# ScalarE's exponential ahead of its copy, and ScalarE writing the outputs of two of the five attention kinds

## What is computed

```python
o_a = _nsa(...)   # 8 heads of 64: per query g0*compressed + g1*selected + g2*window
o_b = _fox(...)   # 8 heads of 64: softmax(q k^T * scale + c_q - c_k) v, "forget gated"
o_m = _memory_xattn(...)   # 4 heads of 128 over 256 memory rows
x = x + (g_0 * (silu * o_a) @ w_a + g_1 * (silu * o_b) @ w_b + g_2 * (silu * o_m) @ w_m) @ w_out
```

## Time and profile before

| | |
|---|---|
| median of 3 runs | 3017.97 us (3016.29 to 3022.12) |
| profiled execution | 3021.99 us, its span 3020.5 us |
| TensorE matmul busy | 2976.1 us (99%) |
| VectorE busy | 1497.1 us (50%) |
| ScalarE busy | 807.1 us (27%) |
| GpSimd busy | 1939.0 us (64%) |
| granted clock, both attention stages | 1.00 |

### The profile page before, as it was taken

One profiled execution on the slowest core, in us unless ns is written; L12 is line 12 of the kernel. 1 busy time (PEld: TensorE's weight loads), 2 busy tenths in 40 slices (PEclk: granted clock), 3 DMA queues, 4 the chain that ended last, 5 costly groups with the idle time before them and its releaser, 6 DMA issues.

```text
span 3020.5 us, 41671 instructions
## 1 busy us (share of the span) xinstructions
PE 2976.1 (99%) x15422; PEld 2495.9 (83%) x15422; DVE 1497.1 (50%) x3021; ACT 807.1 (27%) x1755; POOL 1939.0 (64%) x2192
## 2 busy tenths in 40 slices
PE   9999999999999999999999999999999999999999
PEld 7888887888888878888888887788888988888887
DVE  3333334477730684777213746663334654664332
ACT  1111111322210452222112225552112213564110
POOL 6555554599987788999775862125777684112775
PEclk9999999999999999999999999999999999999999
DMA  4222232122332222323323221011224332011232
GB/s 168 93 90 89 93 105 67 57 98 98 98 98 98 72 82 77 98 98 98 111 91 126 94 95 43 29 36 64 98 98 140 100 103 70 29 43 36 91 98 91
DMA packets 70216, 261.47 MB, mean 87 GB/s; under 512 B 8320, under 2 KB 8832, under 8 KB 68224
## 3 DMA queue, kind: packets, MB, share of 16 engines
q1 hardware_dynamic: 65696, 232.81, 23.6%
q10 hardware_dynamic: 4320, 25.99, 2.4%
HBM read 251.43 MB, written 2.10 MB: 84 GB/s over the span
## 4 chain that ended last, share of the span: by engine, by line
PE 88%; POOL 5%; DVE 3%; issue 2%; ACT 2%; DMA 0%; ACTq 0%; DVEq 0%; SPq 0%; POOLq 0%
PE bank L400 23%; PE bank L402 23%; PE bank L401 23%; POOL w_lo L2314 3%; PE bank L1959 3%; PE bank L1944 1%; PE bank L708 1%; POOL w_hi L2310 1%; PE bank L427 1%; PE bank L440 1%; PE bank L432 1%; PE bank L1660 1%; PE bank L428 1%; PE bank L680 1%; PE bank L1366 1%
## 5 line engine op out<-in xcount | busy, mean ns | idle before, releaser
L2314 POOL TENSOR_TENSOR w_lo<-w_raw,w_hi 128x256 fp32r<-128x256 f32 x1728 | 1406.7, 844 | 36.1
L2310 POOL TENSOR_SCALAR w_hi<-w_raw 128x1024 fp32r<-128x1024 f32 x432 | 489.9, 1134 | 1014.6 <-PE bank L402 918.7
L400 PE MATMUL bank<-in_hi,w_hi 128*128 128x512 f32 x1408 | 554.8, 394 | 0.7 <-POOL w_lo L2314 0.7
L402 PE MATMUL bank<-in_hi,w_lo 128*128 128x512 f32 x1408 | 548.6, 390 | 0.0
L401 PE MATMUL bank<-in_lo,w_hi 128*128 128x512 f32 x1408 | 547.8, 389 | 0.0
L400 PE MATMUL bank<-z_hi,w_hi 128*128 128x512 f32 x976 | 392.4, 402 | 0.4 <-POOL w_lo L2314 0.4
L402 PE MATMUL bank<-z_hi,w_lo 128*128 128x512 f32 x976 | 381.2, 391 | 0.0
L401 PE MATMUL bank<-z_lo,w_hi 128*128 128x512 f32 x976 | 380.7, 390 | 0.0
L402 PEld LDWEIGHTS bank<-in_hi,w_lo 128*128 128x128 f32 x1408 | 264.3, 188 | 56.0
L400 PEld LDWEIGHTS bank<-in_hi,w_hi 128*128 128x128 f32 x1408 | 264.5, 188 | 53.0 <-issue 1.1
L401 PEld LDWEIGHTS bank<-in_lo,w_hi 128*128 128x128 f32 x1408 | 264.7, 188 | 52.8
(11 more groups left out here) (441 smaller groups left out, 5161.5 us busy)
## 6 DMA issues: line engine op xcount, KB each, us to landing
w_raw<-in_units SPq DMA_DIRECT2D x434, 512.0 KB, 3.4
bias<-in_bias ACTq DMA_DIRECT2D x8, 1152.0 KB, 5.1
o_all<-in_cmp_w ACTq DMA_DIRECT2D x4, 2048.0 KB, 8.5
x_res<-in_x ACTq DMA_DIRECT2D x4, 512.0 KB, 7.6
mem_in<-in_mem ACTq DMA_DIRECT2D x2, 1024.0 KB, 8.6
nsa_q_hi<-nsa_q_hi SPq DMA_DIRECT2D x16, 128.0 KB, 2.5
nsa_q_lo<-nsa_q_lo SPq DMA_DIRECT2D x16, 128.0 KB, 2.3
out<-x_res ACTq DMA_DIRECT2D x4, 512.0 KB, 2.6
```

Source lines behind the costliest of these rows:

```text
L400: pe.matmul(out, hi[:, w], rh, start=start and n == 0, stop=False)
L402: last = pe.matmul(out, lo[:, w], rh, start=False, stop=stop and n == len(tiles) - 1)
L2310: d = c.s.unit_hi.on(pool.tensor_scalar(c.w_hi[s][:, :], c.w_raw[s][:, :], 1.0, 0.0, ALU.mult, ALU.add))
L2314: last = pool.tensor_tensor(c.w_lo[s][:, w], c.w_raw[s][:, w], c.w_hi[s][:, w].bitcast(F32), ALU.subtract)
```

## The change

ScalarE's step in `act_attend` now begins with the exponential of task now; the copy of the turned values of task now-2 comes behind it. Behind that copy comes a new instruction where task now-4 is forget-gated or memory: ScalarE itself writes that task's output out of its bank, scaled by the reciprocal of the row sum (`act_store`). VectorE's `dve_store` leaves these 48 tasks of each layer out. A new semaphore, `copied_out`, takes the place of `stored` for them in the three places that wait: the bank's release, the reuse of the small statistics tile (`at_st`) six tasks later, and the transposition of the finished rows (`pe_back`).

```diff
--- before.py
+++ after.py
@@ -85,6 +85,7 @@
         self.w1_loaded, self.mem_loaded = new("cmp_w1_loaded"), new("mem_loaded")
         self.out_stored = new("out_stored")
         self.halves_moved = new("halves_moved")
+        self.copied_out = new("output_copied_out")
         self.piece_hi, self.piece_split = new("piece_hi_by_act"), new("piece_split_by_vector")
 
         self.unit_hi, self.unit_split, self.post_added = new("unit_hi_done"), new("unit_split"), new("post_added")
@@ -1899,7 +1900,7 @@
 
 def pe_back(pe, c, layer, n, j, b):
 
-    pe.wait_ge(*c.s.stored["rows", layer, n, j])
+    pe.wait_ge(*(c.s.copied_out if j else c.s.stored)["rows", layer, n, j])
     pe_free(pe, c, b)
     for i in range(TT):
         m = pe.matmul(c.bank[b][:, i * P:i * P + P], c.o_rows[n % 2][j][:, i, :], c.ident[:, :], is_transpose=True)
@@ -1958,18 +1959,12 @@
     for s, v in enumerate(values):
         m = pe.matmul(o, pt[:, s * P:s * P + P], v, start=s == 0, stop=s == len(values) - 1)
     c.s.weighted.on(m, t.t)
-    c.free[u] = c.s.stored[t.t]
+    c.free[u] = stored(c, t)
 
 
 def act_attend(act, c, layer):
     tasks = tasks_of(layer)
     for now in range(STEPS):
-        if 0 <= now - 2 < TASKS:
-            t = tasks[now - 2]
-            act.wait_ge(*c.s.turned[t.t])
-            if t.index >= 3:
-                act.wait_ge(*c.s.weighted[t.t - 3])
-            c.s.turned_out.on(act.activation(c.at_pt[t.index % 3][:, 0:t.keys], c.bank[3 + t.index % 2][:, 0:t.keys], ACT.Copy), t.t)
         if now < TASKS:
             t = tasks[now]
             st = c.at_st[t.index % 6]
@@ -1983,6 +1978,14 @@
                 m = act.activation(probabilities(c, t)[:, keys], c.bank[t.index % 3][:, keys], ACT.Exp,
                                    scale=exp_scale(c, t, h), bias=st[:, 2 + h:3 + h], accum_out=st[:, 4 + h:5 + h])
             c.s.exponentials.on(m, t.t)
+        if 0 <= now - 2 < TASKS:
+            t = tasks[now - 2]
+            act.wait_ge(*c.s.turned[t.t])
+            if t.index >= 3:
+                act.wait_ge(*c.s.weighted[t.t - 3])
+            c.s.turned_out.on(act.activation(c.at_pt[t.index % 3][:, 0:t.keys], c.bank[3 + t.index % 2][:, 0:t.keys], ACT.Copy), t.t)
+        if 0 <= now - 4 < TASKS and by_act(tasks[now - 4]):
+            act_store(act, c, tasks[now - 4])
         n, step = divmod(now, CHUNK)
         if n < 3 and step == LAST_NSA + 1:
             act.wait_ge(*c.s.logits_ready[tasks[now - 1].t])
@@ -2041,14 +2044,14 @@
     dve.memset(c.fq[0][HD:P, :], 0.0)
     c.s.prepared.on(dve.memset(c.fq[1][0:HD, :], 0.0), ("fox_blank", layer))
     for now in range(STEPS):
-        if 0 <= now - 5 < TASKS:
+        if 0 <= now - 5 < TASKS and not by_act(tasks[now - 5]):
             dve_store(dve, c, tasks[now - 5])
         if now < TASKS:
             t = tasks[now]
             st = c.at_st[t.index % 6]
             dve.wait_ge(*c.s.logits_ready[t.t])
             if t.t >= 6:
-                dve.wait_ge(*c.s.stored[t.t - 6])
+                dve.wait_ge(*stored(c, t, 6))
             bank = c.bank[t.index % 3]
             logits = bank[:, 0:2 * NCP].rearrange("p (g n) -> p g n", n=NCP)[:, :, 0:NC] if t.kind == "cmp" else bank[:, 0:t.keys]
             dmax = step.on(dve.reduce_max(st[:, 0:t.heads], logits, AX_X))
@@ -2116,24 +2119,44 @@
     c.s.lo_done.on(dve.tensor_tensor(c.o_lo[:, n + 4 * j, :], c.o_all[:, n + 4 * j, :], c.o_hi[j][:, n, :].bitcast(F32), ALU.subtract), ("back", layer, n, j))
 
 
+def by_act(t):
+
+    return t.which is None
+
+
+def stored(c, t, back=0):
+    every = tasks_of(t.layer) if t.index >= back else tasks_of(t.layer - 1)
+    t = every[(t.index - back) % TASKS]
+    return (c.s.copied_out if by_act(t) else c.s.stored)[t.t]
+
+
+def act_store(act, c, t):
+    st, o = c.at_st[t.index % 6], c.bank[5 + t.index % 2][:, 0:t.width]
+    kind = {"fox": 1, "mem": 2}[t.kind]
+    act.wait_ge(*c.s.weighted[t.t])
+    act.wait_ge(*c.s.dve_step["factor", t.t])
+    if t.n >= 2:
+        act.wait_ge(*c.s.rows_turned["back", t.layer, t.n - 2, kind])
+    d = c.s.copied_out.on(act.activation(c.o_rows[t.n % 2][kind][:, t.i, t.j * HD:t.j * HD + t.width], o, ACT.Copy, scale=st[:, 8:9]), t.t)
+    c.s.copied_out.value["rows", t.layer, t.n, kind] = d[1]
+
+
 def dve_store(dve, c, t):
     st, o = c.at_st[t.index % 6], c.bank[5 + t.index % 2][:, 0:t.width]
-    kind = {"fox": 1, "mem": 2}.get(t.kind, 0)
+    kind = 0
     out = c.o_rows[t.n % 2][kind][:, t.i, t.j * HD:t.j * HD + t.width]
-    factor = st[:, 8:9] if t.which is None else st[:, 10:11]
+    factor = st[:, 10:11]
     dve.wait_ge(*c.s.weighted[t.t])
     dve.wait_ge(*c.s.dve_step["factor", t.t])
-    if t.n >= 2 and t.kind in ("cmp", "fox", "mem"):
+    if t.n >= 2 and t.kind == "cmp":
         dve.wait_ge(*c.s.rows_turned["back", t.layer, t.n - 2, kind])
     if t.kind in ("sel", "win"):
         dve.wait_ge(*c.s.stored[t.t - 2])
         m = dve.scalar_tensor_tensor(out, o, factor, out, ALU.mult, ALU.add)
-    elif t.kind == "cmp":
+    else:
         def heads(ap):
             return ap.rearrange("p (g d) -> p g d", d=HD)
         m = dve.tensor_tensor(heads(out), heads(o), st[:, 10:12].unsqueeze(2).to_broadcast([P, 2, HD]), ALU.mult)
-    else:
-        m = dve.tensor_scalar(out, o, factor, None, ALU.mult)
     d = c.s.stored.on(m, t.t)
     c.s.stored.value["rows", t.layer, t.n, kind] = d[1]
```

## The result

The changed kernel takes 3032.11 us, the median of 15 runs (3025.29 to 3040.41), against 3021.78 us for the kernel before in the same session (15 runs, 3015.54 to 3022.92). The ratio is 1.0039, with a 95% interval of 1.0029 to 1.005: slower by 0.4%, where 0.2% can be told from no change. It is nearer to the ratio of the means (3031.6 and 3019.8 us) than to that of the medians. The prediction, 3026 us and slower as the likeliest sign, holds the time in its range of 3009 to 3038, which is wide beside an effect of 10 us.

What follows compares the result with a forecast made beforehand. The prediction took TensorE as the bound, 88% of the chain that ended last. Its terms summed to 4.06 us lost a layer, 8 us for two, added to the median of the runs: 3026 us, range 3009 to 3038.

Steps and rivals of the forecast that it cites:

- (a): Tasks 43 to 45, three times a layer: product 44 0.42 us sooner, product 45 0.47 us later, not regained.
- (c): Tasks 49 to 53, three times a layer: copies 50 and 53 behind waiting exponentials, +0.2 us within -0.3 to +0.5.
- (b): Seam of chunks, tasks 58 to 69, three times a layer: gains and delays come to +0.2 us, within -0.1 to +0.5.
- (d): The stage's start, once a layer: copy 3 behind exponential 5 makes product 3 0.9 us late, +0.75 us taken.
- A part is regained from later stalls: At the stage's start: product 3's 0.9 us lateness is partly recovered later, leaving +0.75 us.
- Tasks 12 to 19 of the first chunk: Once a layer: as (a) without the early exponential, +0.7 us.
- The price of the store: Moved store on ScalarE: estimated 312 ns for 64 columns, holding the engine 0.20 us.
- VectorE's relief: VectorE without the moved stores, 48 per layer: about 19 us less busy in the profile after.
- The cover of the statistics tile: VectorE's other work covers its wait to reuse the tile; if the cover is gone, 0.1 to 0.3 us a time.
- Rival 1: VectorE's relief wins: stalls on moved stores go, 12 us gained over two layers, 3006 us; chance 0.15.
- Rival 2: Exponentials don't move, each hanging on the one before through VectorE: 19 us lost, 3037 us; chance 0.2.
- Rival 3: The change does nothing, gains and losses cancel within +/-3 us, 3018 us; chance 0.2.

Runs made afterwards that it cites:

- e1: The kernel before with only ScalarE's order changed, exponential ahead of copy, and VectorE keeping every store: 3033.39 us, ratio 1.0048.
- e7: The changed kernel with the old order, copy ahead of exponential, in the first 12 steps of a layer: 3024.62 us, ratio 1.0017.
- e2: The changed kernel with the copy first again, then exponential, then ScalarE's store, so only the stores are moved: 3027.62 us, ratio 1.0032.
- e3: The stores-only kernel with ScalarE's store moved ahead of the exponential, right behind the copy: 3021.16 us, ratio 1.0006.
- e5: ScalarE's order copy, store, exponential, except the exponential first in step 13 of each chunk: 3016.27 us, ratio 0.9989 against the kernel before.
- e10: As e5, but ScalarE stores only tasks 14, 15 and 26 to 31 of each chunk: 3013.22 us, ratio 0.9994 against the kernel before.
- e4: The kernel before with the exponential ahead of the copy in step 13 of each chunk alone: 3020.41 us, ratio 1.0004.
- e6: The kernel before with 24 more small matmuls on TensorE ahead of layer one's loop: 3020.38 us, ratio 1.0005.

## Why the prediction was right, step by step

The time came out 6 us above the 3026 forecast. The kernel before was itself 3.8 us slower in the 15 runs beside it (3021.78 us) than in the three runs that the forecast started from (3017.97). The two stages account for 1.8 us more than the 8 added, and the rest, under 1 us, isn't told apart from the clock. The mechanism is the one predicted, a copy and a store late behind an exponential. That the sum is as near as 4.06 to 4.98 is in part luck, since its terms erred both ways: too low at the start, in (a), in (c) and at the tail, too high at the seams and in the first chunk.

**(a) Tasks 43 to 45: right, in its details too.** ScalarE of the kernel after, exponential 45 to exponential 48:

```profile
1899.75 0.69 ACT L1978 ACTIVATE at_p<-bank,at_st 128x512 f32<-128x512 f32 x1 [1.24 <-DVE at_st L2071]
...
1900.43 0.58 ACT L1986 ACTIVATE at_pt<-bank 128x512 f32<-128x512 f32 x1
1900.91 0.62 ACT L2022 ACTIVATE fox_q<-o_all 128x512 f32<-128x512 f32 x1
1901.43 0.56 ACT L1978 ACTIVATE at_p<-bank,at_st,mem_scale 128x256 f32<-128x256 f32 x1
...
1901.97 0.28 ACT L1986 ACTIVATE at_pt<-bank 128x128 f32<-128x128 f32 x1
1902.13 0.33 ACT L2140 ACTIVATE o_rows<-bank,at_st 128x64 f32<-128x64 f32 x1
1902.88 0.56 ACT L1978 ACTIVATE at_p<-bank,at_st,mem_scale 128x256 f32<-128x256 f32 x1 [0.42 <-DVE at_st L2071]
...
1903.43 0.58 ACT L1986 ACTIVATE at_pt<-bank 128x512 f32<-128x512 f32 x1
1903.91 0.31 ACT L2140 ACTIVATE o_rows<-bank,at_st 128x64 f32<-128x64 f32 x1
1904.11 0.38 ACT L1978 ACTIVATE cmp_p<-bank,at_st,nsa_scale 128x31 f32<-128x31 f32 x1
```

and TensorE's products 44 and 45:

```profile
1902.67 0.41 PE L1960 MATMUL bank<-fox_v,at_pt 128*128 128x64 f32 x2
...
1904.37 1.08 PE L1960 MATMUL bank<-fox_v,at_pt 128*128 128x64 f32 x8 [0.86 <-ACT o_rows L2140]
```

This is the sequence that the prediction walked through: exponential, copy, tanh, exponential, copy, store. It had exponential 47 at 0.21 us behind product 44 (1905.74 to 1905.95), measured 0.21 (1902.67 to 1902.88); product 45 at 1.66 us behind product 44, measured 1.70. Product 44 gained 0.35 where 0.42 was said, and product 45 came out 0.58 late in net where 0.47 was said (+1.70 at task 43, +2.28 at 45), the same three times: 0.57 from task 69 to 77 and 0.58 from 101 to 109. That is 1.7 us of the 4.98. The reason given was only half of it. The prediction says that store 43 stands behind an exponential and a copy; e1 shows that copy 45 behind exponential 47 costs as much with no store there at all, where VectorE keeps store 42 ahead of maximum 47. So by the timelines the store is in the way once on either engine.

**(b) The seam: smaller than taken.** The prediction took +0.2 in bounds of -0.1 to +0.5. From task 58 to 69 the lateness went from +2.60 to +2.78, 0.18; the seam before it gave -0.05 and the one behind 0.13, 0.26 in sum, not 0.6. The inner steps are there with their signs: 59 loses 0.49 (said 0.45), 60 and 61 lose 0.24 (0.1), 63 gains 0.36 (0.40), 65 loses 0.46 (0.2 to 0.3), 66 and 67 gain 0.19 and 0.34. The longest stall stayed, as said, 0.90 where it was 0.97, behind the same two wide steps of VectorE as in the earlier trace rows. Timeline of the kernel after, VectorE and then TensorE:

```profile
1947.14 0.69 DVE L2119 TENSOR_TENSOR o_lo<-o_all,nsa_o_hi 128x512 fp32r<-128x512 f32 x1 [0.27 <-ACT nsa_o_hi L2000]
1947.75 0.68 DVE L2114 TENSOR_TENSOR o_all<-bank,o_all 128x512 f32<-128x512 f32 x1
1948.35 0.27 DVE L2155 SCALAR_TENSOR_TENSOR o_rows<-bank,at_st,o_rows 128x64 f32<-128x64 f32 x1
```

```profile
1948.78 1.08 PE L1960 MATMUL bank<-win_v,at_pt 128*128 128x64 f32 x8 [0.90 <-DVE o_rows L2155]
```

**(c) Tasks 49 to 53: mis-sized.** Taken at +0.2, within -0.3 to +0.5; measured 0.28 from task 45 to 53 (+2.28 to +2.56) and 0.32 to task 57, with 0.31 and 0.34 in the two chunks behind.

**(d) The start: the term that was most mis-sized.** +0.75 was said and 1.26 measured, confirmed by e7. The prediction priced only copy 3 behind exponential 5, 0.9 us, and that was nearly exact: product 3 was 0.98 late. The even larger lateness of product 1, 1.92, was mostly made good by product 2 (0.43). But behind product 3 nothing came back; tasks 5 to 8 added 0.3 in the same way. TensorE of the kernel after, products of tasks 0, 1 and 3:

```profile
1822.05 0.46 PE L1960 MATMUL bank<-cmp_v,at_pt 128*128 128x128 f32 x2 [0.93 <-issue]
...
1824.47 0.49 PE L1960 MATMUL bank<-cmp_v,at_pt 128*128 128x128 f32 x2 [1.31 <-ACT at_pt L1986]
...
1827.19 1.10 PE L1960 MATMUL bank<-sel_v,at_pt 128*128 128x64 f32 x8 [0.67 <-ACT at_pt L1986]
```

"A part is regained from later stalls" is the sentence that failed. Tasks 12 to 19 of the first chunk gave +0.5 where +0.7 was said. Not foreseen at all was the tail, 0.27 behind task 121 (+4.71 to +4.98). In sum, start 1.26 + first chunk 0.49 + three times 0.58 + 0.97 for (c) + seams 0.26 + tail 0.27 = 4.99, against 4.06 predicted.

**The price of the store: nearly right.** Estimated 312 ns for 64 columns, measured 336; the hold of 0.20 us was exact (1903.91 to 1904.11 above). Groups by shape, kernel after (busy us, mean ns, idle before):

```profile
L2140 ACT ACTIVATE o_rows<-bank,at_st 128x64 f32<-128x64 f32 x32 | 10.8, 336 | 0.0
L2140 ACT ACTIVATE o_rows<-bank,at_st 128x128 f32<-128x128 f32 x16 | 5.9, 368 | 10.9 <-PE bank L1960 10.9
```

The Trainium skill, "ScalarE: Activation LUTs", section "What ACT_TABLE_LOAD costs", gives 186 ns and 0.833 ns a column, with some 93 ns for each operand that is a column of scales: an estimate of 332 ns for 64 columns, and the row agrees with its 336. For 128 columns the same gives 386, and the row has 368. The rule in the Trainium skill's same page, section "Rules for kernel authors", to leave multiplications to VectorE was weighed in the prediction by sign alone, and the runs don't decide it by that sign: with the stores on ScalarE e2 is slower than the kernel before, while e3 and e5, which pay about the same for each (338 and 327 ns), are not. The forecast that ScalarE would be some 30 us busier was wrong (12.4), and VectorE's relief was 15.5 us where 19 was said. The forecast for ScalarE counted whole durations, and each new instruction overlaps its neighbours: in e2, with stores alone, 18 us, and in e1, with the order alone, ScalarE is 6 us less busy.

**The cover of the statistics tile: partly gone.** The prediction priced it at 0.1 to 0.3 us where it fails. VectorE of the kernel after, the maximum of task 49, at a wait for store 43, and the list of such waits over the stage:

```profile
1904.32 0.22 DVE L2057 TENSOR_REDUCE at_st<-bank 128x2 f32<-128x62 f32 x1 [0.54 <-ACT o_rows L2140]
```

```profile
DVE at_st L2057 <- ACT o_rows L2140: 1.6, 3, 0.5
```

Three places of 0.5 us, in each of which ScalarE's store was itself late. Behind the first stands exponential 49 and so part of (c). How much of (c) is due to it wasn't tried, since the wait can't be taken away without another tile.

**The rivals.** Rival 1, VectorE's relief wins, is out: e1 and e2 lose, each alone. Its gain is real only where the place in the queue is right (e3, e5, e10). Rival 2, exponentials don't move, is out: e4 keeps what an earlier one brings, and in e1 and after they start earlier at 44. Rival 3, nothing happens, is out by the ratio, 1.0029 at its lower end.

## What to carry to other kernels

In an engine that works in order, what counts is whose operand the bounding engine wants next, not which engine has time left: put the step that waits longest behind everything that could go meanwhile, unless a row shows that it was ready and stood behind another step's wait, as exponential 45 did. An edit to a loop's order acts at a handful of steps with opposite signs, so keep it only where it gains (one step of 32 gave -1.24 us a layer, all steps +5.70). And before explaining 0.2%, take the clock out of the times.

## What the runs showed of the hardware that I had not expected

TensorE's granted clock fell to half, 1.2 GHz, in a few stretches of every execution, with TensorE busy without a gap ahead of some (the 50 us window above at 0.86) and behind a wait at others. They were 3.4 to 13.7 us long, apart from a shorter one at the end of most spans. The places aren't all chance: each of the twelve profiles has one between 1114 and 1119 us, and the four of the kernel before, e1, e3 and e4 have one of 13.7 us at 1626, which the other eight lack. In the means of a session they cost 5.3 to 12.1 us of a 3 ms span, and the same kernel lost 10.1 us on one occasion and 6.1 on another, which is not clear of the scatter of single executions. That is as much as the change itself, and it hid the gain of e3 and e4 in their ratios (1.0006 and 1.0004, at 1.5 and 2.9 us less net). I found no tie to the number of stalls, and the one shift of the work tried (e6) changed little. What makes them come is left open.

The second: one place in a queue was worth 3.0 us a layer (e2 to e3), with the same 48 stores on the same engine and none of them shorter. It gained at tasks 13, 29, 44 and 49 among others, and lost a part of that again, at 34 and 51.
